# Attention over a prompt: the row maxima reach the query operand by DMA instead of by TensorE and ScalarE

## The reference

```
s = einsum('nqhd,nkhd->nhqk', q, k) * HEAD_DIM ** -0.5          # 16 heads of 64
s = s + (c_q[..., None] - c_k[..., None, :])                     # c = cumsum of log forget values
s = where(k_pos <= q_pos, s, NEG_INF)
p = softmax(s, axis=-1)                                          # stable: the row maximum is taken off
out = einsum('nhqk,nkhd->nqhd', p, v)
```

## Time and profile before

| | us |
|---|---|
| median of 3 runs | 2558.7 (2558.35 to 2562.17) |
| profiled execution | 2559.47 |
| its span, first to last instruction | 2557.1 |
| PE, DVE, ACT, POOL busy in the span | 2525.0, 1809.3, 1050.5, 24.4 |
| the sweep over the prompt's heads | from about 1412 to 1690 us of the span |

### The profile page before, as it was taken

How to read it: one execution, slowest core, us unless ns; L and a number is a source line. 1 busy time by engine, 2 the same in 40 slices (tenths; PEclk the granted TensorE clock), 3 DMA queues, 4 the chain that set the end, 5 groups by cost and what they waited for, 6 DMA issues and landing times.

```text
span 2557.1 us, 45942 instructions
## 1 busy us (share of the span) xinstructions
PE 2525.0 (99%) x18332; PEld 2472.9 (97%) x18332; DVE 1809.3 (71%) x2446; ACT 1050.5 (41%) x1502; POOL 24.4 (1%) x48
## 2 busy tenths in 40 slices
PE   8999999999999999999999999999999999999998
PEld 8999999999999999999999899988899999999998
DVE  5434437666688998954345898876596666899986
ACT  4111124333333323465245777765563333333233
POOL 0000000000000000000000100000000000000000
PEclk9999999999999999999999999999999999999999
DMA  3111111333353312025324556634323332533112
GB/s 120 50 41 49 42 43 38 126 101 101 101 198 102 126 69 84 10 85 167 110 79 138 144 136 167 147 121 146 94 86 105 101 101 101 186 135 120 67 52 69
DMA packets 249038, 259.42 MB, mean 101 GB/s; under 512 B 18144, under 2 KB 184192, under 8 KB 248898
## 3 DMA queue, kind: packets, MB, share of 16 engines
q1 hardware_dynamic: 229638, 248.37, 31.1%
q10 hardware_dynamic: 19260, 9.09, 1.3%
HBM read 193.86 MB, written 63.42 MB: 101 GB/s over the span
## 4 chain that ended last, share of the span: by engine, by line
PE 88%; DVE 3%; DMA 3%; ACT 2%; SPq 2%; issue 1%; ACTq 0%; DVEq 0%
PE ps L595 28%; PE ps L807 24%; PE ps L862 24%; PE ps L827 2%; DMA sums_spread<-o_and_sums 1%; PE ps L1271 1%; PE ps L1186 1%; PE ps L1121 1%; PE ps L1272 1%; PE ps L1273 1%; PE ps L1188 1%; PE ps L1479 1%; PE ps L646 1%; PE ps L709 1%; SPq L1574 0%
## 5 line engine op out<-in xcount | busy, mean ns | idle before, releaser
L862 PE MATMUL ps<-h_op,w_op 128*128 128x268 f32 x4912 | 614.2, 286 | 0.2
L862 PEld LDWEIGHTS ps<-h_op,w_op 128*128 128x128 f32 x4912 | 609.5, 188 | 0.7 <-DVE w_op L902 0.6
L595 PE MATMUL ps<-x_hi,w_hi 128*128 128x358 f32 x1248 | 280.5, 330 | 2.2 <-DVE x_lo L626 1.2
L595 PE MATMUL ps<-x_hi,w_lo 128*128 128x358 f32 x1248 | 276.2, 327 | 0.0
L595 PE MATMUL ps<-x_lo,w_hi 128*128 128x358 f32 x1248 | 275.6, 327 | 0.0
L579 DVE TENSOR_TENSOR w_lo<-w_raw,w_hi 128x1024 fp32r<-128x1024 f32 x76 | 92.8, 1221 | 251.3 <-ACT w_hi L571 251.3
L873 ACT ACTIVATE w_op<-w_op_f 128x2048 fp32r<-128x2048 f32 (+1 forms) x54 | 97.6, 1808 | 382.3 <-PE ps L862 361.5
L595 PEld LDWEIGHTS ps<-x_hi,w_hi 128*128 128x128 f32 x1248 | 214.0, 189 | 5.0 <-DVE x_lo L626 1.8
L595 PEld LDWEIGHTS ps<-x_lo,w_hi 128*128 128x128 f32 x1248 | 216.4, 189 | 0.0
L595 PEld LDWEIGHTS ps<-x_hi,w_lo 128*128 128x128 f32 x1248 | 216.1, 189 | 0.0
L1059 DVE TENSOR_TENSOR t<-ps,t 128x536 f32<-128x536 f32 x180 | 128.7, 715 | 120.3 <-PE ps L807 111.4
(11 more groups left out here) (364 smaller groups left out, 5180.3 us busy)
## 6 DMA issues: line engine op xcount, KB each, us to landing
raw_a<-in_mlp_w SPq DMA_DIRECT2D x120, 256.0 KB, 3.1
h_op_f<-h_rows SPq DMA_DIRECT2D x24, 1072.0 KB, 6.2
w_op_f<-in_mlp_w SPq DMA_DIRECT2D x24, 1024.0 KB, 7.4
h_rows<-t SPq DMA_DIRECT2D x90, 268.0 KB, 2.1
w_raw<-in_conv_w_in SPq DMA_DIRECT2D x24, 512.0 KB, 3.8
w_raw<-in_w_kv SPq DMA_DIRECT2D x16, 512.0 KB, 4.9
w_raw<-in_w_o SPq DMA_DIRECT2D x16, 512.0 KB, 3.9
k_page<-in_cache_k SPq DMA_DIRECT2D x16, 512.0 KB, 5.0
```

Source lines behind the costliest of these rows:

```text
L595: mm = pe.matmul(PS[:, bank(s, g), 0:GW], w[:, s, k], x[:, k, g * GW:(g + 1) * GW], start=(k == 0 and n == 0), stop=(k == KC - 1 and n == 2))
L862: mm = pe.matmul(PS[:, 2 * p + g, 0:QW], w[:, k, P * m:P * m + P], x[:, k, QW * g:QW * g + QW], start=(k == 0 and j == 0), stop=(k == tile ...
```

## The change

- The uses "A", "B", "C" leave the list, so that 13 passes are left. The new table `USE_AT` puts three small ones in g = 0, two in g = 1 to 3, one in g = 4 and 5, two in g = 6 and none in g = 7. The join of B comes in g = 3, that of C in g = 6.
- PE's one-column matmuls and ScalarE's copies are gone. `move_shift` issues one DMA per tile (four for A, three for B, two for C) from a column of `NMR` straight into the row of `QA`; the minus sign goes to the key operand's row, set to -1.
- `logits` waits for these DMAs (`nm_in`); `ring_wait` waits for reductions alone. Two of the three semaphores are reused ones, with offsets.
- SP's list per head is now: C(h); in odd heads `load_v`; `load_cross(h + 1)`; staging and cache pages (three `load_logf` in heads 8 to 12, one in head 13; one `load_k` in heads 9 to 12); `spread_sums(h - 1)`; A(h + 1); `load_head(h + 2)`; B(h + 1); `load_inverse(h - 1)`.
- Head 0's maxima are moved by DMAs that ScalarE issues. `late_norm` takes its bank from the ring.

```diff
 USES = ["M", (1, 0, 144), (2, 0, 272), (3, 0, 400), (4, 16, 528), (5, 0, 512), (5, 512, 656), (6, 0, 512), (6, 512, 784),
-        "A", (7, 0, 512), "B", (7, 512, 912), (8, 16, 528), (8, 528, NPR), "C"]
+        (7, 0, 512), (7, 512, 912), (8, 16, 528), (8, 528, NPR)]
...
+SHIFT_COUNT = {"A": 64, "B": 48, "C": 32}
+SHIFT_IN = {"A": 0, "B": 16, "C": 16}
...
-JOIN_AT = {3: "A", 8: "B", 14: "C"}
-USE_AT = [(0, 1), (2, 3), (4, 5), (6, 7), (8, 9), (10, 11), (12, 13), (14,)]
-USE_AT_FIRST = [(), (0, 1, 2), (3, 4, 5), (6, 7)] + USE_AT[4:]
-NORM_HEAD, NORM_BANK, NORM_USE = 1, 5, 13
-SHIFT_AT = {4: "A", 5: "B"}
-FIRST_USES = [(), (), (), (0, 1, 2, 3), (4, 5, 6, 7), (8, 9, 10, 11), (12, 13, 14), (15,)]
+JOIN_AT = {3: "A", 8: "B", 12: "C"}
+USE_AT = [(0, 1, 2), (3, 4), (5, 6), (7, 8), (9,), (10,), (11, 12), ()]
+USE_AT_FIRST = [(), (0, 1, 2), (3, 4, 5), (6, 7, 8)] + USE_AT[4:]
+NORM_HEAD, NORM_USE = 1, NUSE - 2
+FIRST_USES = [(), (), (), (0, 1, 2, 3), (4, 5, 6, 7), (8, 9), (10, 11, 12), ()]
...
-            return (4 if h else 6) + u % RING
+            return 4 + (NUSE * h + u) % RING if h else 6 + u % RING
...
-            if USES[u0] in SHIFTS:
-                pe.wait_ge(nm_kept, N_SH * h0 + "ABC".index(USES[u0]) + 1)
-            else:
-                pe.wait_ge(red_done, reds_through(h0, u0))
+            pe.wait_ge(red_done, reds_through(h0, u0))
...
-        def keep_shift(h, x):
-
-            u = USES.index(x)
-            q0, q1 = max_rows(SHIFTS[x][0])[0], sum(max_rows(SHIFTS[x][-1]))
-            act.wait_ge(mx_done, NUSE * h + u + 1)
-            act.activation(QA[h % SETS][HD:HD + 1, q0:q1], PS[0:1, bank_of(h, u), 0:q1 - q0], ACT.Copy, scale=-1.0)\
-               .then_inc(nm_kept, 1)
+        def move_shift(eng, h, x):
+
+            _, hh = head(h)
+            eng.wait_ge(nm_ready, N_SH * h + "ABC".index(x) + 1)
+            to = QA[h % SETS][HD:HD + 1].bitcast(F32)
+            for i in SHIFTS[x]:
+                q, rows = max_rows(i)
+                eng.dma_start(to[:, q:q + rows].rearrange("o (p i) -> o p i", i=1), NMR[0:rows, hh, i:i + 1].bitcast(F32))\
+                   .then_inc(nm_in[x], 16)
...
-                pe.wait_ge(nm_kept, N_SH * h + CHUNK_OF[g] + 1)
+                x = "ABC"[CHUNK_OF[g]]
+                pe.wait_ge(nm_in[x], SHIFT_IN[x] + SHIFT_COUNT[x] * (h + 1))
...
             def prompt_loads():
                 for h in range(HEADS):
                     if h:
+                        move_shift(sp, h, "C")
+                        if h % 2 == 1 and h + 1 < HEADS:
+                            load_v(h // 2 + 1)
                         if h + 1 < HEADS:
                             load_cross(h + 1)
-                        if h + 2 < HEADS:
-                            load_head(h + 2)
+                        if h == 4:
+                            stage_out(2 * KC - 2)
...
+                        if 8 <= h < 8 + DB * NPAGE // 3 + 1:
+                            for x in range(3 * (h - 8), min(3 * (h - 8) + 3, DB * NPAGE)):
+                                load_logf(x)
+                        if 9 <= h < 9 + 2 * NPAGE:
+                            load_k((h - 9) // NPAGE, [(h - 9) % NPAGE])
                         spread_sums(h - 1)
+                    if h + 1 < HEADS:
+                        move_shift(sp, h + 1, "A")
+                    if 0 < h and h + 2 < HEADS:
+                        load_head(h + 2)
+                    if h + 1 < HEADS:
+                        move_shift(sp, h + 1, "B")
+                    if h:
                         load_inverse(h - 1)
-                    if h % 2 == 0 and h + 2 < HEADS:
-                        load_v(h // 2 + 1)
...
-            pool.memset(CK[n][HD:HD + 1].bitcast(F32), 1.0).then_inc(ext_ready, 1)
+            pool.memset(CK[n][HD:HD + 1].bitcast(F32), -1.0).then_inc(ext_ready, 1)
```

More of the change, by code:

```diff
@@ L195 @@
 SHIFTS = {"A": range(0, 4), "B": range(4, 7), "C": range(7, NT)}
-REDS = [0 if x in SHIFTS else 2 if x == "M" else 1 for x in USES]
+SHIFT_COUNT = {"A": 64, "B": 48, "C": 32}
+SHIFT_IN = {"A": 0, "B": 16, "C": 16}
+REDS = [2 if x == "M" else 1 for x in USES]
 N_RED, N_SH = sum(REDS), len(SHIFTS)
-JOIN_AT = {3: "A", 8: "B", 14: "C"}
-USE_AT = [(0, 1), (2, 3), (4, 5), (6, 7), (8, 9), (10, 11), (12, 13), (14,)]
-USE_AT_FIRST = [(), (0, 1, 2), (3, 4, 5), (6, 7)] + USE_AT[4:]
-NORM_HEAD, NORM_BANK, NORM_USE = 1, 5, 13
-SHIFT_AT = {4: "A", 5: "B"}
-FIRST_USES = [(), (), (), (0, 1, 2, 3), (4, 5, 6, 7), (8, 9, 10, 11), (12, 13, 14), (15,)]
+JOIN_AT = {3: "A", 8: "B", 12: "C"}
[3 more added lines that the diff above has]
+FIRST_USES = [(), (), (), (0, 1, 2, 3), (4, 5, 6, 7), (8, 9), (10, 11, 12), ()]
 RING = 2
@@ L494, in trunk @@
         logf_stored, c_stored = sem("logf_stored"), sem("c_stored")
+        nm_in = {"A": sem("nm_in"), "B": gate_w_loaded, "C": bf_loaded}
         lt_kept = sem("lt_kept")
@@ L1100, in max_logits @@
             ring_wait(h, u)
[L1101 to L1110, removed]
+            if u == 0 and NORM_HEAD + 1 < h <= NORM_HEAD + 1 + G:
+                pe.wait_ge(aux_read, AX_Q + 3 * (KC - 1) + h - NORM_HEAD - 1)
+            if x == "M":
                 for j, i in enumerate(FIRST_KEYS):
@@ L1744, in attention_scalar @@
             values_hi(0)
-            keep_shift(0, "C")
+            move_shift(act, 0, "C")
             exp_logits(1)
@@ L1750, in attention_scalar @@
                 if g == 1 and NORM_HEAD < h <= NORM_HEAD + G:
-                    root(AX_Q + 3 * (KC - 1) + h - NORM_HEAD - 1, NORM_BANK, h - NORM_HEAD - 1)
-                h, g = divmod(t - 1, NG)
-                if 0 <= h < HEADS - 1 and g in SHIFT_AT:
-                    keep_shift(h + 1, SHIFT_AT[g])
-                if 0 < h < HEADS - 1 and g == 0:
-                    keep_shift(h, "C")
-                elif h == HEADS - 2 and g == NG - 1:
-                    keep_shift(h + 1, "C")
+                    root(AX_Q + 3 * (KC - 1) + h - NORM_HEAD - 1, bank_of(h, NORM_USE), h - NORM_HEAD - 1)
                 h, g = divmod(t - 2, NG)
@@ L1999, in late_norm @@
             c = slice(g * GW, (g + 1) * GW)
-            pe.matmul(PS[:, NORM_BANK, 0:GW], heads1[:, :], SQ[U_Q][1][1][:, c], start=True, stop=False)
-            pe.matmul(PS[:, NORM_BANK, 0:GW], heads1[:, :], T2R[:, c], start=False, stop=True).then_inc(aux_done, 1)
+            b = bank_of(NORM_HEAD + g + 1, NORM_USE)
+            pe.matmul(PS[:, b, 0:GW], heads1[:, :], SQ[U_Q][1][1][:, c], start=True, stop=False)
+            pe.matmul(PS[:, b, 0:GW], heads1[:, :], T2R[:, c], start=False, stop=True).then_inc(aux_done, 1)
         def uses_at(h):
@@ L2012, in uses_of @@
                 return uses + [h - NORM_HEAD]
-            if g == 0 and 0 < h < HEADS - 1:
-                return [(h, last_shift)] + uses
-            if g == NG - 1 and h == HEADS - 2:
-                return uses + [None, (h + 1, last_shift)]
             return uses
@@ L2647, in _ @@
                 if n == 5:
-                    keep_shift(0, "A")
-                    keep_shift(0, "B")
+                    move_shift(act, 0, "A")
+                    move_shift(act, 0, "B")
                 head_root(ax(AX_Q + 3 * n, 0, 0), n == KC - 2)
@@ L3330, in norm @@
                         pe.wait_ge(red_done, reds_through(0, FIRST_USES[n][-1]))
-                        pe.wait_ge(nm_kept, sum(USES[u] in SHIFTS for u in range(FIRST_USES[n][-1] + 1)))
                     f()
```

26 lines of the change are left out of this document (7 added, 19 removed).

## The result

The change makes the kernel slower: 2589.4 us (2586.1 to 2592.5, five runs) against 2560.9 us (2558.4 to 2562.2, five runs) for the kernel before on the same chip, a ratio of 1.0115 (95% interval 1.0104 to 1.0126), or +28.5 us. The forecast was 2573 us, the range 2550 to 2600. The direction was right and the size was half of what came.

What follows compares the result with a forecast made beforehand. The prediction took TensorE, busy 99% of the span, as the bound. Ordinary heads +4.5, heads 9 to 12 +12, head 8 +1.5, spread sums -3 and first head -1 made +14 us: 2573 us, range 2550 to 2600.

Steps and rivals of the forecast that it cites:

- The issue cost: SP's nine small DMAs per head: 0.6 us each to issue, with 0.35 and 0.9 as ends.
- the third pass: Third small pass in a head's first group: PE waits 1.3 us for VectorE's first small reductions, with the inverse late.
- heads 9 to 12: Heads where SP also loads cache pages: maxima and inverse land late, +3 us for each of the four, 12 us.
- SP's new order: SP's list per head: spread sums go ahead of the next head's load, partly relieving VectorE's waits, -3 us.
- at full granted clock: TensorE in the sweep: busy 99% at full clock, so whatever leaves its stream counts unless another engine sets the pace.
- the removed matmuls: Nine one-column transposes per head on PE: 0.8 us saved per head, 12.5 us over 16 heads.
- smaller terms: Outside the main waits: head 8 +1.5 us, spread sums partly relieved -3 us, first head -1 us.
- Values for the next head: ScalarE waits 2 us for later-loaded values; costed at nothing, covered by PE's g0 wait; uncovered up to 8 us.
- Ordinary heads: Heads 1 to 7, 13 and 14: -0.8 + 1.3 = +0.5 us each, +4.5 us for nine.
- The reload: Inverse sums behind B in SP's queue: reload starts at S + 12.85 instead of S + 12.0, landing 3.9 us later.
- rival 3: SP sets the pace at 0.9 us per issue: about +42 us, 2601 us; chance 0.20.

Runs made afterwards that it cites:

- The run with the pages late: The changed kernel with the cache pages loaded behind the inverse's reload instead of ahead of the spread sums: 2587.2 us, 1.0117.
- the run with the values early: The changed kernel with values loaded at the end of the even heads' list, a head before they are split, as before: 2587.5 us, 1.0115.
- late wait and free division: Changed kernel, copies to an unread SBUF row, PE waiting two groups later, logits scaled to a hundredth, division not awaiting the inverse in 14 heads: 2577.5 us.
- the new order alone: The kernel before with the changed kernel's list order for SP, without any of the nine copies: 2556.0 us, 0.9990.
- doubling: The kernel before with each of the nine one-column matmuls per head issued twice: 2562.9 us, 1.0020.
- The changed kernel with the late wait: The changed kernel, copies to an unread SBUF row, PE waiting for them two groups later, exponentials of a hundredth of the logits: 2587.0 us, 1.0109.
- the kernel before with the copies: The kernel before with the changed kernel's SP list and nine copies per head to an unread SBUF row, nobody waiting: 2595.1 us, 1.0143.

## Why the forecast was half of it

**What held.** The issue cost (0.60 us), the waits and their order, the third pass (1.6 us against 1.3), that heads 9 to 12 carry most of it, and the reasons: the inverse and the maxima queue behind each other on SP. SP's new order does no harm, which the forecast also had (a small gain).

**The step that failed: the clock was put at nothing.** The forecast began "at full granted clock" and gave no term to what becomes of the clock when PE stands. The rest of its sum came out nearly right, in all though not in each part. Its +14 us hold the removed matmuls 14 times at 0.8, so its waits and smaller terms make 14 + 11.2 = 25 us; PE stands for 28 us more in the sweep. The matmuls' 0.8 us per head is the 0.77 by which PE's busy time fell. What is left is the lower clock: some 14 us in the sweep, and half of 6.8 us behind it. In heads 9 to 12 it shows most, before and after:

```profile
1573.10:1641.81 68.71, 66.62 (x486) 62.50 (x485) 58.21 (x149) 50.57 (x101) 0.00 (x0) 1.00 0.64 158
1580.86:1665.49 84.63, 72.36 (x449) 69.14 (x449) 59.46 (x148) 46.40 (x89) 0.00 (x0) 0.88 0.55 129
```

There 12.2 us of waits were forecast (12 - 3, and 4 x 0.8 for the matmuls) and PE stands for 10.2 us more; but it is also busy for 5.7 us more, with fewer matmuls, and 20.5 us are at the lower level.

This is where the time lies, not what a full clock would give back. Where PE is late after a slow stretch, it waits less at the next wait. The run with the pages late has 17 us at the lower clock in its sweep, the run with the values early 31, and both take the changed kernel's time. With late wait and free division 17 us are left, with the new order alone none. No run takes the clock away and keeps the waits.

**The transposes are not settled.** By their starts they were worth 0.77 us per head, by PE's busy time 0.77, by doubling 0.3. The changed kernel with the late wait and the kernel before with the copies have the same list for SP with the same unread copies, and are 8 us apart; the transposes, ScalarE's row copies and the placement of the passes are together in those 8. Were the gain only the 4.4 us of the doubling, the sum would be 14 + 8 = 22.

**Values for the next head, costed at nothing.** The step said that PE's wait in the first group covers them, and up to 8 us without the cover. They are 13.5 us of ScalarE's waits in the changed kernel. Loading them earlier gave nothing back, so there they are covered; with the other waits gone they grow to 32 us. What of these the kernel's time pays was not measured.

**Ordinary heads.** +0.5 was forecast and +1.0 came in heads 1 to 4: 0.77 less for the matmuls, and 1.7 more of standing, not 1.3. The reload comes later than taken. With S = 1469.29, the start of the value products in head 3, it is issued at S + 15.2 instead of S + 12.85, because A's maxima are ready at S + 6.0 and not 4.7, B's three copies take 2.65 us in this head and not 1.9, and the reload can go 1.56 us behind the store instead of 1.35.

**Which rival.** It is nearest to rival 3, SP sets the pace, with a time between it (2601) and the forecast; but by another way. That rival asked for 0.9 us per issue; 0.6 was measured. SP's list fits into a head in sum, as the forecast had it, yet it is in order: it stands still for the maxima while the values and the store behind them are due. In the changed kernel the store follows B's last copy by 0.04 to 0.25 us in fourteen heads; in the kernel before SP stood idle for 4.7 to 8.1 us ahead of it.

**What stays open.** The 19 us left when neither the copies nor the inverse are waited for were not divided further between values, next head's operands and clock. With ScalarE issuing the copies SP's list is that of before, and 25 us are left; PE's waits for the maxima are 13 of it at most, and the rest has no run of its own. One DMA for several tiles' maxima, which would cut the issues from nine to three, was not tried. Of all versions only the kernel before in the new order is level with it; no run beats it by what the measurement can tell.

## What to carry to other kernels

Moving a small job from a busy engine to DMA trades engine time for time on an in-order queue: count the issues and the standing in front of them, and compare the two with the idle time that the queue has just ahead of its most urgent entry, not with its idle share over a period. Where waits are added to an engine at full clock, the forecast needs a term for the clock; here it was as large as the forecast itself. Doubling a part prices one more of it, not its removal: the two differed by more than a factor of two here. And a control must keep the kind of transfer: unread copies to DRAM cost some 200 us, to SBUF 39.

## What the runs showed of the hardware

- A copy of 128 elements of 4 bytes, one from each partition, into one SBUF row takes its issuing engine 0.60 us (0.47 to 1.38) and lands 2.5 us after the issue (1.7 to 5.3). Into a DRAM row it lands after 8.2 us (median), and 512 KB loads in the same queue then take 11.2 us instead of 4.0.
- In the changed kernel PE stands for 1.1 to 2.5 us once or twice in most heads, and its clock falls from 2.4 to 1.2 GHz six times in the sweep of 297 us, for 3.4 to 10.2 us each and 30.7 us in all. Each fall comes within 1.4 us of the end of such a stand (1.7 to 2.5 us long); stands of 2.1 us (to 1545.05) and 2.4 us (to 1599.67) brought none. In the sweep of the kernel before, where the longest stand is 0.8 us, there is no fall.
- A reload that waits until its 4 KB store has landed in DRAM is issued 1.3 us behind the store where SP had stood idle ahead of it, and 2.3 us behind it (median, 1.3 to 3.2) in the changed kernel, where the store directly follows other issues.
